# Splitting raw projection weights on GpSimd beside the stick-breaking heads, with all large tiles at one remainder

## What is computed

```python
h = layer_norm(x, ln0_g, ln0_b)
proj = jnp.einsum('btd,dc->btc', h, w_in[l])            # 1024 x 4096
qa, ka, va, qb, kb, vb, gate = jnp.split(proj, split_at, axis=-1)
ya = dilated_mixture(heads_a(qa), heads_a(ka), heads_a(va), rel_bias)   # 8 heads, 3 dilations, bias on logits
yb = stick_breaking(heads_b(qb), heads_b(kb), heads_b(vb))             # 8 heads
y = jnp.concatenate([ya, yb], axis=-1) * jax.nn.silu(gate)
out = jnp.einsum('btc,cd->btd', y, w_out[l]) + b_out[l]
h = layer_norm(DEEPNORM_ALPHA * h + out, ln_g[l], ln_b[l])

# stick-breaking: A[t,s] = sigmoid(z_ts) * prod_{s<j<t} (1 - sigmoid(z_tj)), s < t; out = A v
# dilated branch: s = q.k / 8 + rel_bias[bucket(distance)], band of 128 steps, softmax
```

## Time and profile before

| what | us |
|---|---|
| median of 3 runs (1655.92 to 1660.64) | 1658.01 |
| the profiled execution | 1657.32 |
| its span | 1655.5 |
| TensorE busy | 1616.5 |
| VectorE busy | 1132.4 |
| ScalarE busy | 721.4 |
| GpSimd busy | 414.0 |

### The profile page before, as it was taken

How to read it: one execution, slowest core, us unless ns; L and a number is a source line. 1 busy time by engine, 2 the same in 40 slices (tenths; PEclk the granted TensorE clock), 3 DMA queues, 4 the chain that set the end, 5 groups by cost and what they waited for, 6 DMA issues and landing times.

```text
span 1655.5 us, 26798 instructions
## 1 busy us (share of the span) xinstructions
PE 1616.5 (98%) x9102; PEld 1375.0 (83%) x9102; DVE 1132.4 (68%) x2188; ACT 721.4 (44%) x1788; POOL 414.0 (25%) x260
## 2 busy tenths in 40 slices
PE   5999999999999999999999999999999999999997
PEld 4777888888888888888888888887999999988886
DVE  5731124322226888888888898888678787878887
ACT  5541113201214555555555555555676767641000
POOL 2202100000000111111111111113478778771232
PEclk9999999999999999999999999999999999999999
DMA  5337856545659564946494648442657677555542
GB/s 188 143 119 261 308 219 222 205 141 171 207 184 297 174 204 132 294 140 197 137 290 140 194 135 251 142 151 80 182 147 212 163 213 198 150 187 195 164 154 77
DMA packets 185358, 305.01 MB, mean 184 GB/s; under 512 B 52185, under 2 KB 109076, under 8 KB 180436
## 3 DMA queue, kind: packets, MB, share of 16 engines
q1 hardware_dynamic: 180756, 294.01, 56.2%
q0 software_dynamic: 2400, 9.48, 1.7%
q10 hardware_dynamic: 2080, 0.01, 0.1%
HBM read 190.38 MB, written 108.73 MB: 181 GB/s over the span
## 4 chain that ended last, share of the span: by engine, by line
PE 83%; DVE 6%; issue 4%; DMA 2%; ACT 2%; SPq 1%; POOL 1%; DVEq 0%; POOLq 0%; ACTq 0%
PE proj L398 25%; PE proj_a L1086 14%; PE out_ps L1911 7%; PE wt_ps L1055 7%; PE oa_ps L1475 6%; PE o_ps L1071 4%; PE o_ps L1069 4%; PE z_ps L1045 3%; PE z_ps L1044 3%; PE pt_ps L1456 3%; PE s_ps L1447 3%; PE s_ps L1448 2%; DVE WT_lo L1174 1%; SPq L1365 1%; PE vtp L398 1%
## 5 line engine op out<-in xcount | busy, mean ns | idle before, releaser
L1119 ACT ACTIVATE WT_hi<-wt_ps 128x512 fp32r<-128x512 f32 (+1 forms) x320 | 171.1, 535 | 298.6 <-PE wt_ps L1055 298.4
L1166 DVE TENSOR_TENSOR_SCAN W<-w,W,zeros 128x512 f32<-128x512 f32 x192 | 257.3, 1340 | 44.2 <-ACT w L1111 42.4
L398 PE MATMUL proj<-h_hi,w_hi 128*128 128x512 f32 x608 | 246.9, 406 | 4.5 <-DVE h_lo L578 3.3
L398 PE MATMUL proj<-h_lo,w_hi 128*128 128x512 f32 x608 | 241.0, 396 | 0.0
L398 PE MATMUL proj<-h_hi,w_lo 128*128 128x512 f32 x608 | 240.8, 396 | 0.0
L1509 ACT ACTIVATE prob<-neg_s,rows 128x256 f32<-128x256 f32 (+1 forms) x384 | 173.5, 453 | 89.9 <-DVE rows L1556 89.2
L1174 DVE TENSOR_TENSOR WT_lo<-wt_ps,WT_hi 128x512 fp32r<-128x512 f32 (+1 forms) x320 | 187.1, 585 | 2.2 <-ACT WT_hi L1119 2.2
L1055 PE MATMUL wt_ps<-ident,W 128*128 128x128 f32 x1088 | 174.0, 275 | 6.5 <-DVE WT_lo L1174 5.4
L1023 POOL TENSOR_TENSOR y_sum<-y_sum,ends 64x512 f32<-64x512 f32 x32 | 34.4, 1074 | 563.6 <-DVE y_sum L1181 563.6
L1111 ACT ACTIVATE w<-z_ps 128x512 f32<-128x512 f32 (+2 forms) x320 | 169.2, 529 | 8.1 <-PE z_ps L1045 8.1
L1055 PEld LDWEIGHTS wt_ps<-ident,W 128*128 128x128 f32 x1088 | 130.6, 140 | 45.1 <-DVE WT_lo L1174 18.4
(11 more groups left out here) (198 smaller groups left out, 3168.2 us busy)
## 6 DMA issues: line engine op xcount, KB each, us to landing
wa_hi<-wa_d SPq DMA_DIRECT2D x48, 512.0 KB, 4.0
wa_lo<-wa_d SPq DMA_DIRECT2D x48, 512.0 KB, 5.0
wa_d<-x_sb SPq DMA_DIRECT2D x24, 512.0 KB, 3.7
va_d<-st SPq DMA_DIRECT2D x48, 256.0 KB, 2.6
va<-va_d SPq DMA_DIRECT2D x12, 1024.0 KB, 8.4
w_raw<-in_w_tiles SPq DMA_DIRECT2D x18, 512.0 KB, 5.0
x_sb<-in_x SPq DMA_DIRECT2D x16, 512.0 KB, 5.7
qk_hi_d<-st SPq DMA_DIRECT2D x32, 256.0 KB, 2.4
```

The lines of the kernel that those rows point to most:

```text
L398: last = pe.matmul(acc_of(n)[:], w[w_slot(t)][:, k, :], h[ch][:, k, :], start=(k, a) == (0, 0), stop=(k, a) == (KD - 1, 2))
L1119: act.activation(WT_hi[n % PART_SLOTS][:, cols], t_ps[n % T_SLOTS][:, cols], ACT.Copy) \
L1166: dve.tensor_tensor_scan(W[n % W_SLOTS][:, 0:width][:, ::-1], w[n % W_IN][:, 0:width][:, ::-1], above[:, ::-1], first, ALU.mult, ALU.max). ...
```

## The change

1. **Weights split in the stage.** The front no longer touches the 12 late tiles. SP loads each raw tile into one buffer `wa_raw`, the next when the split before it is done. GpSimd casts it into wa_hi and subtracts into wa_lo, behind `a_done` of the group that used the slot. TensorE waits for `wa_split` in place of the load. `wa_d` is gone.
2. **Order on GpSimd.** Splits 0 and 1 stand ahead of the three clearings, the others between the y work of the query blocks: ahead of block n's go those whose slot comes free by step LAST[n] + 14.
3. **Bias.** The row is stored reversed, once per head (`toe_d`, 3 x 8 x 384). A load reads 128 rows of 256 values, each one element further on, straight from it. The minima read it backwards (`[:, ::-1]`).
4. **Places.** Fillers (`gap_before_w`, `gap_before_h`, `gap_before_wo` and changed `gap_...`) put all large tiles of all stages at remainder 384 to 512 bytes; o_low moves. VectorE waits at step 8 for the last stores of the front, since tiles now overlap the store buffers.

```diff
-        A_AT, A_SLOTS = (36, 38, 40, 42, 44, 46, 66, 68, 70, 72, 74, 76), 4
...
+        m.sb("gap_before_w", [P, 56])
         w_raw = m.sb("w_raw", [P, KD, P])
...
-                pool.dma_start(toe_row_d[c], x_sb[3 + c][0:HEADS, 0:TOE]).then_inc(toe_sent, 16)
...
+                pool.dma_start(toe_d[c], x_sb[3 + c][0:HEADS, 0:TOE]).then_inc(toe_sent, 16)
...
-                if n in A_AT:
-                    a = A_AT.index(n)
-                    act.wait_ge(wa_loaded[a % A_SLOTS], 16 * (a // A_SLOTS + 1))
-                    act.activation(wa_slot(a, 1).bitcast(F32R), wa_slot(a, 0), ACT.Copy).then_inc(wa_hi_done, 1)
...
+            row = toe_d[c, bass.ds(head, 1), 1:TOE]
+            sp.dma_start(self.bias[par][:, c, :], bass.AP(row.tensor, row.offset, [[1, P], [1, 2 * P]])) \
+                .then_inc(self.bias_loaded[par], 16)
...
+        m.sb("gap_weights", [P, 512])
+        wa_raw = m.sb("wa_raw", [P, KD, P])
...
-                if a >= 2:
-                    sp.wait_ge(a_done, a - 1)
-                for part, tile in enumerate((wa_hi, wa_lo)):
-                    sp.dma_start(tile[a % 2][:].bitcast(F32), wa_d[a % A_TILES, part]).then_inc(wa_loaded[a % 2], 16)
+                if a >= 1:
+                    sp.wait_ge(wa_split, a)
+                sp.dma_start(wa_raw[:], w_tiles[W_TILES + a % A_TILES]).then_inc(wa_loaded, 16)
...
+            def split_wa(a):
+                pool.wait_ge(wa_loaded, 16 * (a + 1))
+                if a >= 2:
+                    pool.wait_ge(a_done, a - 1)
+                pool.tensor_copy(wa_hi[a % 2][:], wa_raw[:]).then_inc(wa_hi_done, 1)
+                pool.wait_ge(wa_hi_done, a + 1)
+                pool.tensor_tensor(wa_lo[a % 2][:], wa_raw[:], wa_hi[a % 2][:].bitcast(F32),
+                                   ALU.subtract).then_inc(wa_split, 1)
+
+            pool.wait_ge(*front.toe_free)
+            split_wa(0)
+            split_wa(1)
+            pool.wait_ge(wa_split, 2)
             pool.wait_ge(front.w_split, front.w_tiles)
             for slot in range(Q_SLOTS):
                 pool.memset(q_lo0[slot][DH:P, :].bitcast(F32), 0.0).then_inc(q_zeros_set, 1)
+            pool.wait_ge(q_zeros_set, Q_SLOTS)
+            split = 2
             for n in range(GROUPS):
+                if n >= 1:
+                    pool.wait_ge(y_done, n)
+                while split < A_GROUPS and A_END[split - 2] + 1 <= LAST[n] + VALUES_LAG + 3:
+                    split_wa(split)
+                    split += 1
+                pool.wait_ge(wa_split, split)
...
-                        pe.wait_ge(wa_loaded[a % 2], 32 * (a // 2 + 1))
+                        pe.wait_ge(wa_split, a + 1)
...
+                if s == LOW_LAG:
+                    for landed, count in front.stores:
+                        dve.wait_ge(landed, count)
...
-                        in1=bias[par][:, c, (2 - nk) * P:2 * P], scale=-SCALE, scalar=3e38,
+                        in1=bias[par][:, c, 0:nk * P][:, ::-1], scale=-SCALE, scalar=3e38,
```

More of the change, by code:

```diff
@@ L263, in settle @@
             sp.wait_ge(h_stored, 16 * 4)
-            for slot in range(A_SLOTS):
-                sp.wait_ge(wa_stored[slot], 32 * A_TILES // A_SLOTS)
         @block.sync
@@ L651, in _, with __init__ @@
                     second(n)
[L652 to L658 removed]
+        toe_free = (toe_sent, 16 * 3)
+        return FrontEnd(m.semaphores, close, settle, second_done, len(GROUPS), h_stored, toe_free, w_split, W_TILES,
+                        [(st_stored[slot], stored_by(len(GROUPS) - ST_SLOTS + slot)) for slot in range(ST_SLOTS)])
 class FrontEnd:
[L664 removed]
+    def __init__(self, spent, close, settle, second_done, groups, h_stored, toe_free, w_split, w_tiles, stores):
         self.spent, self.close, self.settle = spent, close, settle
@@ L979, in _ @@
             plan(A_END[A_TILES * (NCH - 1) + 4] + 8, load_first, NCH)
-            for slot in range(3):
-                sp.wait_ge(front.wa_stored[slot], front.wa_counts)
+            sp.wait_ge(*front.toe_free)
             load_wa(0)
+            load_wa(1)
             load_k(0, 0)
-            sp.wait_ge(front.wa_stored[3], front.wa_counts)
             load_q(0)
             sp.dma_start(ones_above[:], mask).then_inc(mask_loaded, 16)
-            load_wa(1)
             load_k(0, 1)
@@ L1543, in _ @@
             dve.sem_inc(gated, 2)
+            dve.wait_ge(*stick.results)
             def minima(it, b):
```

80 lines of the change are left out of this document (19 added, 61 removed).

## The result

The changed kernel takes 1717.97 us, median of 4 runs (1713.66 to 1721.13), against 1657.36 us of the kernel before (4 runs, 1655.92 to 1660.64): ratio 1.0363, 95% interval 1.0337 to 1.0388. That is 61 us slower; the forecast was 12 us slower. The profiled execution took 1721.13 us with a span of 1719.2.

A forecast was written before the change was run, and what follows sets the result against it. TensorE, busy for 98% of the span, was taken as the bound. The terms -12.4 - 8 - 1 + 4.4 + 3 + 23 + 3 gave +12 us, so 1669 us, with an 8-in-10 range of 1642 to 1694.

The forecast's parts named there:

- Front -12.4: Front: equal start remainders of weights and activations shorten its matmuls, -12.4 us, between 0 and -12.8.
- The rule: Large matmul tiles: operands at unequal remainders to 512 bytes cost about 6.6 ns a matmul, equal ones nothing.
- Stick-breaking stage -8 by the remainder: Stick-breaking stage: equal remainders shorten value and projection matmuls, -8 us, between -3 and -11, if VectorE keeps up.
- Output -1: Output stage: 12 matmuls per token tile on the two odd weight slices get shorter, -1 us.
- Leaving the front, the bias: 0: Front and dilated stage: work leaving the front, and bias by overlapping rows and backward read, change time by 0 us.
- Start of the stage +4.4 and +3: Stick-breaking stage's start: TensorE waits for the first splits and GpSimd's clearings, +4.4 us; a further +3, between 0 and 4.
- The scans lose 1.6 us a split: Stick-breaking stage: GpSimd's splits hold off VectorE's scans, 1.6 us for each of 46, bounds 0.9 and 2.4.
- TensorE feels 0.5 of each, +26 with the old pairs: Stick-breaking stage: each split costs TensorE 0.5 us, +23 us (bounds 5 and 45), and +3 for the earlier GpSimd pairs.
- VectorE becomes the bound: Rival, stick-breaking stage: at 2.4 us a split VectorE's work of 683 us exceeds the stage; 1690 us, chance 0.13.
- Late splits 0: Stick-breaking stage: raw weights load and split in 9.1 us against a period of 13.7, so waiting for them costs 0 us.
- that rival: Stick-breaking stage: SP holds the raw load behind a wait for y, TensorE stands for wa_split; 1684 us, chance 0.06.
- The dilated stage 0: Dilated stage: no loss expected, the new bias loads and backward read being covered by VectorE's spare time, 0 us.

The follow-up runs named there:

- the first two runs: Kernel before with a 56-word filler ahead of the front's weight tiles, then the same plus the whole bias change: 1649.43 and 1649.46 us.
- The run with four strokes: Changed kernel with loads and cast on GpSimd and each split's subtraction on VectorE, cut in four behind successive steps: 1685.29 us.
- the filler alone: Kernel before with only a 56-word filler ahead of the front's weight tiles, so they start at remainder 320 like h: 1649.43 us.
- an eighth and a half: Changed kernel with GpSimd's cast and subtraction covering one eighth, or one half, of each weight tile from the third on: 1662.96 and 1680.64 us.

## Why the prediction was wrong

It had the direction and three of its mechanisms (the front, the output, the lock between scan and subtraction), and 49 us too little; 1718 lies outside its range. In the profiled execution, at 1721.13 us, it is 52: 31 in the stick-breaking stage (+56.1 against +25.4), 20 in the dilated stage and 2 in the front.

- *Front -12.4*: -10.6. Right in place and nearly in size: from the start of the front's last 360 matmuls to that of the stage's first one are 81.7 us, as forecast. The rule was too narrow. A remainder of 256 beside 320 should have gained nothing and gained 7.5 us.
- *Stick-breaking stage -8 by the remainder*: 0. Take the distance from each matmul's start to the next one's, the median for each pair of kinds, and add it up over the stage: 644.0 us before and 644.9 after. The matmuls of the values, whose dv moved, gained 1.6 us (157.7 to 156.1), the others lost 2.5. This is a step that failed, 8 us; why the values gained 1.6 us in place of 4 stays open.
- *Output -1*: -1.3; the 528 matmuls of the chain take 119.99 us against 121.06, and the gain lies in the 12 per token tile that it named.
- *Leaving the front, the bias: 0*: right, shown by the first two runs. That the backward read costs nothing shows in its 421 ns of mean before and after.
- *Start of the stage +4.4 and +3*: 2.1 us of wait for GpSimd's clearing. No run shows the +3 as a loss of time: no half clock stands behind that wait in this execution, and in seven of the later kernels 3.4 or 6.8 us of it begin between 500.9 and 502.5 us. Together too large by 5 us.
- *The scans lose 1.6 us a split*: 1.44, right, and the lock of the earlier trace rows is what happens: the scan beside the subtraction takes 3.39 us in place of 1.27. The cast reads SBUF too and costs the scans only 5 to 16 us in all.
- *TensorE feels 0.5 of each, +26 with the old pairs*: the step that failed most. VectorE's loss of 62 us became 56 us of stage, 0.9 of each microsecond in place of 0.35. I took the stalls of before, behind losses of 0.34 us that mostly vanished, and let VectorE win back a tenth. It did not: its waits for w, which were to fall from 78 to below 20 us as it used them up, stayed at 72.9, and it is idle for 80 us of the longer stage against 86 before. Even its own work costs 0.65 to 0.69. The clock behind TensorE's stands was priced at the start only; the 17.1 us at half clock in the stage may be up to 8.5 of the 56 (estimate). The rival "VectorE becomes the bound" came nearest for this stage (+7.4 and +38) but for another reason: it asked for 2.4 us a split, 1.44 were measured, and VectorE is busy 635 of 716 us.
- *Late splits 0*: wrong as a reading of the load's timing, 18.5 us of waits with SP behind y as that rival said. Their price stays open: without them the stage is no shorter, but its scans lose 15.5 us more.
- *The dilated stage 0*: +19.6, seen by no step and no rival. I had written that a longer dilated stage would speak for the backward read; it spoke for the place of VectorE's loop in its program.

Why VectorE's idle eighth absorbs so little stays open. The run with four strokes does not settle whether it is the length of its strokes, since VectorE stood for the cast in it. `deal` gives TensorE its share of projection in proportion to VectorE's time in each step, which leaves no step with much room; that was not tried with another table.

## What to carry to other kernels

Where two engines exclude each other, cut the instruction of the one that has time: four subtractions in place of one took 50 us off this stage. Do not credit one edit with the whole: that kernel stands level with the one before only because a filler had won 10 us in the front, and the filler alone is better. A side engine's average idle time says little about what it can lose: VectorE was idle for 86 us of the stage, and 62 us more of its time made 56 us of stage. Price a loss by an experiment with a known dose, an eighth and a half. Hold each run against the one that differs from it by one edit. After any edit look at the loops as well, on every engine whose program became longer or shorter: a gap put down to "issue" at a loop's turn went with packets of kind "instruction" here (2.38 us with two, 4.68 with three), and eleven instructions fewer cost 14 us.

## What the runs showed of the hardware

- A loop's turn costs VectorE 2.3 to 2.8 us where the record has two packets of kind "instruction" (22 turns in eleven kernels, for instance 2.44 and 2.38) and 4.6 to 5.2 us where it has three (12 turns in six kernels, for instance 4.68 and 5.16); with the cast on ScalarE the counts are four and six. Each of these packets is 8 KB (60 of them are 0.49 MB on the page of the kernel before). The kernel before shifted by 117 instructions and the changed kernel, shifted by -11, both have three. The two places are 128 instructions apart, so a pattern that repeats every 128 instructions would fit; that is an estimate from two places.
- A stand of TensorE of 1.5 to 2.1 us was followed by 10 to 14 us at half clock in each of the 12 loop turns that had one, and at the 22 turns without one the clock did not fall.
- Matmuls of 128x512 with F32R operands, remainders to 512 bytes: in the front 0.2333 us with weights at 96 or 288 and h at 320, 0.229 with 256 and 320, 0.227 with both at 320 or 384; in the output stage 0.2333 with 320 and 128, 0.227 with both at 128 or 384. No rule tried here covers all of them.
- A GpSimd subtraction of 128x1024 and a VectorE scan exclude each other: 3.39 us for a scan of 1.27. In four pieces the 46 splits took 24 us from the scans in place of 82.
